# Expert choice: router logits from rows not normed yet, and the first gather issued a stage earlier

## The chip, the cores and the metric

One core of a Trainium2 chip runs the whole program in one launch. The metric is the device time of one execution in microseconds (us). The median of three runs stands for a kernel; one further execution was profiled.

## The reference, cut to what matters

The program is a model of a first block and a second block of two layers. All is float32; there are 1024 tokens of 1024 features. Each layer of the second block ends in this:

```
x   = layer_norm(ALPHA * x + mix, ln_mix_g, ln_mix_b)      # mix = a @ w_o
aff = softmax(x @ w_router, axis=-1)                       # 1024 x 16
gates, idx = top_k(aff.T, 128)                             # 128 tokens for each of 16 experts
out = silu(x[idx] @ w_g) * (x[idx] @ w_u) @ w_down * gates
ffn = zeros.at[idx].add(out)
x   = layer_norm(ALPHA * x + ffn, ln_ffn_g, ln_ffn_b)
```

The last product of the mixing, `a @ w_o`, the first layer norm, the router and the choice of tokens are one stage of the kernel. The experts are the next.

## The kernel before, in words

`layer_tail` runs twice, as `ec0` for the first layer and as `ec1` for the second. It calls `product_and_choose` (names `ec0p`, `ec1p`) and then `choice_phase` (`ec0e`, `ec1e`). Each is a block of its own: every engine has its own list of instructions in a fixed order, engines wait for each other by semaphores, and all engines meet at the end of a block.

**product_and_choose** goes over 8 tiles of 128 tokens. For tile t:

- TensorE makes the product in two halves of 512 columns (`product`, L2840), eight float32 matmuls each, which the trace shows as 16 records. Between them it transposes the previous tile's normed rows `o` (`transposes`, L2849) and, from tile 2 on, turns the affinities of the tile before that (`turn_aff`, L2867). After the second half it makes the previous tile's router logits (`logits`, L2860).
- VectorE adds the residual (`total`, L2963), norms (`normed`, L2969 to L2983), does the softmax (`softmax`, L2988 to L2993) and keeps the turned affinities (`keep_aff`, L2999).
- ScalarE squares and roots (`square_and_root`), does the Exp (`exps`), copies the transposed rows out of PSUM (`keep_x`, L2923), and issues the stores of `o` and of ALPHA times `o` (`store_o`, `store_acc`). It loads the Exp table and the Sqrt table in turn.
- SyncE loads the residual rows, the norm's vectors, the router's weight, and then the first expert's weights.

The choice of the 128 best tokens is made by 16 rounds of MAX8 and MATCH_REPLACE8 on VectorE (`rounds`, L3007 to L3013), once over tokens 0 to 511 (part 0) and once over the rest (part 1). Part 0 runs in the later tiles, part 1 after the last tile, and then the two lists are merged (L3042 to L3047), transposed by TensorE (L2887, L2888) and cast into `idx` (L3050).

In stretches where TensorE would be idle, `stay_awake` (L35) multiplies an identity matrix by itself: 15 times ahead of the last tile's transposes, 22 times near the end of part 1's rounds, and 16 times at the start of `choice_phase`.

**choice_phase** first copies a column of `idx` and gathers 128 rows of x with an indirect DMA issued by GpSimd (`gather`, L3116). TensorE, after its 16 identity matmuls, transposes them (`turn_x`, L3162), VectorE copies all 1024 columns out of PSUM (`keep_x`, L3303), and the loop over experts begins (L3183).

Of the kernel before, what the change touches and what calls it, by code (L numbers as in the profile page):

```python
# [74 lines left out]
class Phase:  # L75
# [27 lines left out]
    def engine(self, eng, name):  # L103
# [12 lines left out]
            lru_lambda_2=16)  # L116
# [2614 lines left out]
class Layers:  # L2731

    def __init__(self, ph, ahead):
# [10 lines left out]
        self.tile_out = ph.sem("tile_out")  # L2744


def layer_tail(nc, outer, name, layers, wo_in, ln_mix, w_router, w_gu, w_dn, x_dram, mid_dram, acc_dram, ln_ffn, out_dram, steps, end):

    with Phase(nc, name, into=outer) as ph:
        gate = ph.sb("gate", [P, E2])  # L2750
        idx = ph.sb("idx", [P, E2], U32)
        weights = Experts(ph, w_gu, w_dn, layers.wd)
        with Phase(nc, f"{name}p") as one:
            product_and_choose(nc, one, layers, layers.aT, layers.ident, wo_in, ln_mix, w_router, x_dram, mid_dram, acc_dram, gate, idx, weights, ln_ffn,
                               steps, end)
        choice_phase(nc, ph, f"{name}e", layers, mid_dram, acc_dram, gate, idx, weights, ln_ffn, out_dram, steps, end)


def product_and_choose(nc, ph, layers, aT, ident, wo_in, ln_mix, w_router, x_dram, mid_dram, acc_dram, gate, idx, weights, ln_ffn, steps, end):
# [7 lines left out]
    junk = ph.sb("junk", [P, D])  # L2767
    warm = ph.sb("warm", [P, NT + 1])
    xT = ph.sb("xT", [P, 2, KD, P])
    small = ph.sb("small", [P, 2, 8])  # L2770
# [16 lines left out]
    def lanes(part, n):  # L2787
# [8 lines left out]
             "a_kept acc_ready tops f_psum cleared near_end").split()  # L2796
    (consts, half_psum, summed, nm_ready, sq_done, ms_ready, root, o_half, x_psum, xT_ready, l_psum, sh_ready, exp_done, aff_ready, a_psum,
     a_kept, acc_ready, tops, f_psum, cleared, near_end) = [ph.sem(n) for n in names]
# [6 lines left out]
    with nc.Block() as block:  # L2805

        @block.sync
        def _(sp):
# [23 lines left out]
        def _(pe):  # L2832

            def product(t, h):
                if t == 0:
                    pe.wait_ge(wo_in[h], 32)
                if t >= 2:
                    pe.wait_ge(summed, 2 * (t - 2) + h + 1)
                for k in range(KD):
                    m = nc.tensor.matmul(po[:, t % 2, halves[h]], aT[:, k, t * P:(t + 1) * P], wo[:, k, halves[h]], start=k == 0, stop=k == KD - 1)  # L2840
                m.then_inc(half_psum, 1)

            def transposes(t):
                for h in range(2):
                    pe.wait_ge(o_half, 2 * t + h + 1)
                    if t:
                        pe.wait_ge(xT_ready, 2 * (t - 1) + h + 1)
                    for k in range(4 * h, 4 * h + 4):
                        m = nc.tensor.transpose(pt[:, k * P:(k + 1) * P], o[:, t % 2, k * P:(k + 1) * P], ident[:, :])  # L2849
                    m.then_inc(x_psum, 1)  # L2850

            def logits(t):
                if t == 0:
                    pe.wait_ge(consts, 48)
                else:
                    pe.wait_ge(exp_done, t)
                for k in range(KD):
                    if k % 4 == 0:
                        pe.wait_ge(xT_ready, 2 * t + k // 4 + 1)
                    m = nc.tensor.matmul(pl[:, 0:E2], xT[:, t % 2, k, :], w[:, k, :], start=k == 0, stop=k == KD - 1)  # L2860
                m.then_inc(l_psum, 1)
# [7 lines left out]
            for t in range(NT):  # L2869
                product(t, 0)  # L2870
                if t >= 2:
# [11 lines left out]
            pe.wait_ge(exp_done, NT)  # L2883
# [7 lines left out]
        @block.gpsimd  # L2891
        def _(pool):
            for part in range(2):
                nc.gpsimd.memset(top[part][:, :], 0.0)
                for j in range(PER):
                    m = nc.gpsimd.memset(state[part][j], 0.0)
                m.then_inc(cleared, 1)

        @block.scalar
        def _(act):  # L2900
# [8 lines left out]
            def exps(t):  # L2909
                u = t % 2  # L2910
                act.wait_ge(sh_ready, t + 1)
                if t >= 2:
                    act.wait_ge(aff_ready, t - 1)
                nc.scalar.activation(ex[:, u, :], pl[:, 0:E2], ACT.Exp, bias=soft[:, u, 0:1], accum_out=soft[:, u, 1:2]).then_inc(exp_done, 1)
                if t < NT - 1:
                    nc.scalar.activation(warm[:, t:t + 1], ident[:, 0:1], ACT.Sqrt)

            def keep_x(t):
                for h in range(2):
                    act.wait_ge(x_psum, 2 * t + h + 1)  # L2920
                    if t >= 2:
                        act.wait_ge(l_psum, t - 1)
                    nc.scalar.copy(xT[:, t % 2, 4 * h:4 * h + 4, :], pt[:, halves[h]].rearrange("p (k t) -> p k t", k=4)).then_inc(xT_ready, 1)  # L2923
# [11 lines left out]
            for t in range(NT):  # L2935
                square_and_root(t)
                if t:
                    exps(t - 1)
                store_o(t)
                if t < NT - 1:  # L2940
                    store_acc(t)
                keep_x(t)
            nc.scalar.activation(warm[:, NT - 1:NT], ident[:, 0:1], ACT.Exp)
            exps(NT - 1)
            store_acc(NT - 1)
# [8 lines left out]
        def _(dve):  # L2954
# [11 lines left out]
            def normed(t):  # L2966
# [3 lines left out]
                dve.wait_ge(nm_ready, t + 1)  # L2970
                if t >= 2:
                    dve.wait_ge(o_out[u], 16 * (t // 2))
                    dve.wait_ge(x_psum, 2 * (t - 1))
                    dve.wait_ge(acc_ready, t - 1)
                if t == 0:
                    dve.wait_ge(consts, 48)
# [5 lines left out]
                for h in range(2):  # L2982
                    nc.vector.scalar_tensor_tensor(o[:, u, halves[h]], o[:, u, halves[h]], small[:, u, 6:7], gb[:, 1, halves[h]], ALU.mult, ALU.add).then_inc(o_half, 1)  # L2983

            def softmax(t):
                u = t % 2
                dve.wait_ge(l_psum, t + 1)
                nc.vector.reduce_max(soft[:, u, 0:1], pl[:, 0:E2], AX_X, negate=True).then_inc(sh_ready, 1)  # L2988
# [4 lines left out]
                nc.vector.tensor_scalar(aff[:, :], ex[:, u, :], soft[:, u, 2:3], None, ALU.mult).then_inc(aff_ready, 1)  # L2993

# [21 lines left out]
            between = {5: (range(0, 0), range(0, 6)), 6: (range(6, 9), range(9, 12)), 7: (range(12, 14), range(14, 16))}  # L3016
            total(0, 0)
            total(0, 1)
            for s in range(1, NT + 1):
                if s > 1:  # L3020
                    total(s - 1, 1)
                normed(s - 1)
                if s >= 2:
                    softmax(s - 2)
                if s in between and between[s][0]:
                    rounds(0, between[s][0])
                if s < NT:
                    total(s, 0)
                if s >= 2:
                    keep_aff(s - 2)  # L3030
                if s in between and between[s][1]:
                    rounds(0, between[s][1])
# [16 lines left out]
            for g in range(NGR):  # L3049
                nc.vector.tensor_copy(idx[32 * g:32 * g + WIDE, 0:E2], pl[0:WIDE, 32 * g:32 * g + E2])  # L3050


def choice_phase(nc, outer, name, layers, x_dram, acc_dram, gate, idx, weights, ln_ffn, out_dram, steps, end):
# [13 lines left out]
    with Phase(nc, name, into=outer) as ph:  # L3067
        wg, wd, wg_in, wd_in = weights.wg, weights.wd, weights.wg_in, weights.wd_in
        ic = [ph.sb(f"ic{v}", [P, 1], U32) for v in range(2)]
        xg = ph.sb("xg", [P, D])  # L3070
# [11 lines left out]
        names = "ic_ready x_in x_psum x_ready g_used half_psum silu hid_ready h_psum hT_a hT_v d_used y_ready sent added".split()  # L3082
        (ic_ready, x_in, x_psum, x_ready, g_used, half_psum, silu, hid_ready, h_psum, hT_a, hT_v, d_used, y_ready, sent,
# [8 lines left out]
        with nc.Block(no_gpsimd_drain=True) as block:  # L3092
# [19 lines left out]
            def _(pool):  # L3112
# [6 lines left out]
                pool.wait_ge(ic_ready, 2)  # L3119
                gather(0)  # L3120
# [34 lines left out]
            def _(pe):  # L3155
# [11 lines left out]
                turn_x()  # L3167
# [53 lines left out]
            def _(act):  # L3221
# [39 lines left out]

                with act.Fori(0, LAST) as e:
# [34 lines left out]
            def _(dve):  # L3297
                V.open(hT_v, x_ready, y_ready)
                V.open(hid_ready, n=2)
                dve.wait_ge(x_psum, 2)  # L3300
# [3 lines left out]

                keep_x()
# [484 lines left out]
def moe_and_transformer_kernel(nc, I, out):  # L3790
# [10 lines left out]
    with ExitStack() as routes:  # L3801
# [23 lines left out]
        with Phase(nc, "layers") as both:  # L3825
            layers = Layers(both, ahead)
# [39 lines left out]
```

## Time and profile before

| | |
|---|---|
| median of 3 runs | 4438.68 us (4438.11 to 4441.31) |
| the profiled execution | 4434.76 us, its span 4433.0 us |
| mean granted TensorE clock | 0.986 |
| busy share of the span | TensorE 96%, its weight loads 50%, VectorE 35%, ScalarE 24%, GpSimd 6% |
| part of the chain that ended last | TensorE 15% of the span, all else near 0% |

Times in the profile count from the start of the span. A busy TensorE is one with matmuls under way; float32 matmuls appear as two records each, and records overlap, so the distance between starts says more than a record's own length.

### The profile page before, as it was taken

What the parts mean: (1) busy time and instruction counts of PE and PEld (TensorE: products, weight loads), DVE (VectorE), ACT (ScalarE), POOL (GpSimd) and SP (SyncE); (2) the same over time, 40 slices, a digit from 0 to 9 for tenths busy, and PEclk for the clock granted to TensorE, in tenths of its full rate; (3) what the DMA queues carried; (4) which work ended last, traced back from release to release, by engine and by line L of the source; (5) the groups of instructions that cost most, each with busy time, mean ns of one, the idle gap of its engine ahead of it and who ended that gap; (6) DMA issues with size and microseconds to landing.
All of it is one profiled execution on the core that took longest, in us unless ns stands there. A gap on an engine that the chain in (4) does not pass through costs nothing. (4 is left out here: it accounts for less than half of the span.)

```text
span 4433.0 us, 62622 instructions
## 1 busy us (share of the span) xinstructions
PE 4248.5 (96%) x23844; PEld 2232.4 (50%) x23845; DVE 1561.6 (35%) x2869; ACT 1083.2 (24%) x1861; POOL 276.7 (6%) x326
## 2 busy tenths in 40 slices
PE   9999999998999999989898899999999997999998
PEld 6555446777445644454554444444444454444443
DVE  4564564443432422233756201010456444011013
ACT  1364223444210011111643000000346331000002
POOL 0000002221000010010000000000000000000000
PEclk9999999999999999999999999999999998999999
DMA  2300155332322699940114688989511144988896
GB/s 87 149 27 31 43 214 131 91 91 64 132 100 84 221 361 360 347 167 19 39 68 185 224 314 314 319 306 318 173 35 34 62 185 175 317 307 321 308 321 244
DMA packets 411747, 807.84 MB, mean 182 GB/s; under 512 B 140944, under 2 KB 276112, under 8 KB 378640
## 3 DMA queue, kind: packets, MB, share of 16 engines
q1 hardware_dynamic: 382496, 704.01, 45.5%
q0 software_dynamic: 16848, 61.35, 4.7%
q10 hardware_dynamic: 12192, 39.46, 2.2%
q8 instruction: 158, 2.59, 0.2%
q14 instruction: 53, 0.43, 0.0%
HBM read 682.77 MB, written 121.63 MB: 181 GB/s over the span
## 5 line engine op out<-in xcount | busy, mean ns | idle before, releaser
L3183 PE MATMUL ec1e_pg<-ec_wg,ec1e_xT 128*128 128x512 f32 x1024 | 443.8, 594 | 2.1 <-DVE ec1e_xT L3303 2.1
L3183 PE MATMUL ec0e_pg<-ec_wg,ec0e_xT 128*128 128x512 f32 x1024 | 442.1, 592 | 2.1 <-DVE ec0e_xT L3303 2.1
L3183 PEld LDWEIGHTS ec1e_pg<-ec_wg,ec1e_xT 128*128 128x128 f32 x1024 | 195.1, 191 | 247.8 <-issue 247.8
L3183 PEld LDWEIGHTS ec0e_pg<-ec_wg,ec0e_xT 128*128 128x128 f32 x1024 | 194.5, 190 | 246.7 <-issue 246.7
L3211 PE MATMUL ec0e_py<-late_wd,ec0e_hidT 128*128 128x512 f32 x512 | 226.2, 594 | 3.4 <-ACT ec0e_hidT L3239 3.4
L3211 PE MATMUL ec1e_py<-late_wd,ec1e_hidT 128*128 128x512 f32 x512 | 226.2, 594 | 3.4 <-ACT ec1e_hidT L3239 3.4
L3539 PE MATMUL lrui_pA<-lrui_xT,lrui_w 128*128 128x512 f32 x512 | 221.3, 592 | 1.4 <-DVE lrui_xT L3692 1.4
L785 PE MATMUL front_pz<-h_h_all,h_w 128*128 128x512 f32 x480 | 209.5, 594 | 3.2 <-PEq L91 3.2
L3234 ACT ACTIVATE ec1e_sg<-ec1e_pg 128x512 f32<-128x512 f32 x32 | 19.1, 597 | 599.0 <-PE ec1e_pg L3183 599.0
L3234 ACT ACTIVATE ec0e_sg<-ec0e_pg 128x512 f32<-128x512 f32 x32 | 19.1, 597 | 598.8 <-PE ec0e_pg L3183 598.8
L3311 DVE TENSOR_TENSOR ec1e_hid<-ec1e_sg,ec1e_pg 128x512 f32<-128x512 f32 x32 | 22.0, 688 | 399.5 <-ACT ec1e_sg L3234 399.5
L3311 DVE TENSOR_TENSOR ec0e_hid<-ec0e_sg,ec0e_pg 128x512 f32<-128x512 f32 x32 | 22.0, 688 | 398.3 <-ACT ec0e_sg L3234 398.3
L3539 PEld LDWEIGHTS lrui_pA<-lrui_xT,lrui_w 128*128 128x128 f32 x512 | 97.2, 190 | 124.2 <-issue 124.2
L1124 POOL TENSOR_TENSOR wkv_a_l<-wkv_a_raw,linear_tab 128x512 f32<-128x512 f32 x80 | 106.4, 1361 | 791.1 <-ACT wkv_a_raw L1143 791.1
L3211 PEld LDWEIGHTS ec0e_py<-late_wd,ec0e_hidT 128*128 128x128 f32 x512 | 94.7, 190 | 113.9 <-issue 113.9
L3211 PEld LDWEIGHTS ec1e_py<-late_wd,ec1e_hidT 128*128 128x128 f32 x512 | 94.7, 190 | 113.9 <-issue 113.9
L785 PEld LDWEIGHTS front_pz<-h_h_all,h_w 128*128 128x128 f32 x480 | 90.5, 190 | 120.2 <-issue 120.2
L534 PE MATMUL mlaa_pS<-mla_kT,mla_qT 96*128 96x512 f32 x256 | 123.8, 606 | 6.5 <-ACT mlaa_probs L598 4.5
L1337 PE MATMUL wkv_bZ<-h_h_all,h_w 128*128 128x512 f32 x240 | 126.6, 612 | 1.5 <-PEq L91 1.5
L3568 PE MATMUL lrui_pB<-late_wd,lrui_gw 128*128 128x512 f32 x256 | 116.4, 613 | 6.5 <-ACT lrui_buf L3608 6.5
L2840 PE MATMUL ec1p_po<-late_wd,layers_aT 128*128 128x512 f32 x256 | 112.7, 594 | 1.7 <-PEq L91 1.7
L2840 PE MATMUL ec0p_po<-late_wd,layers_aT 128*128 128x512 f32 x256 | 112.7, 594 | 1.7 <-PEq L91 1.7
(690 smaller groups left out, 6446.6 us busy)
## 6 DMA issues: line engine op xcount, KB each, us to landing
ec_wg<-in_moe_w_gate_up_dram SPq DMA_DIRECT2D x256, 1024.0 KB, 6.7
late_wd<-in_moe_w_down_dram SPq DMA_DIRECT2D x256, 512.0 KB, 4.5
moe_wb<-in_w_dram SPq DMA_DIRECT2D x32, 1024.0 KB, 12.1
h_h_all<-in_w_dram SPq DMA_DIRECT2D x32, 1024.0 KB, 11.9
yb<-mlaa_zero SPq DMA_DIRECT2D x1, 16384.0 KB, 43.1
moe_w2b<-in_w_dram SPq DMA_DIRECT2D x16, 1024.0 KB, 12.2
mixed_mixT<-in_w_dram SPq DMA_DIRECT2D x16, 1024.0 KB, 12.4
yb<-ahead_rows ACTq DMA_DIRECT2D x32, 512.0 KB, 7.8
```

The source lines that it names most:

```text
L534: m = nc.tensor.matmul(pS[:, u % 2 * 2 + j, :], q_all[:, head, tile * P:(tile + 1) * P], k_all[:, head, j * HALF:(j + 1) * HALF], start=Tr ...
L785: m = nc.tensor.matmul(pz[q % 2][:, half * HALF:(half + 1) * HALF], w[:, q % U, k, :], hT[:, k, half * HALF:(half + 1) * HALF], start=k == ...
L1124: nc.gpsimd.tensor_tensor(grid(a_l[:, n, :]), grid(a_raw[:, :]), mask(n + 1), ALU.mult).then_inc(a_masked, 1)
L1337: m = nc.tensor.matmul(bZ[:, :], gate_w[:, slot, k, :], hT[:, k, halves[g % 2]], start=k == 0, stop=k == KD - 1)
L2840: m = nc.tensor.matmul(po[:, t % 2, halves[h]], aT[:, k, t * P:(t + 1) * P], wo[:, k, halves[h]], start=k == 0, stop=k == KD - 1)
L3183: return nc.tensor.matmul(pg[:, b, :], xT[:, k, :], wg[:, k, b * HALF:(b + 1) * HALF], start=k == 0, stop=k == KD - 1)
L3211: m = nc.tensor.matmul(py[:, b * HALF:(b + 1) * HALF], hidT[:, k, :], wd[:, k, b * HALF:(b + 1) * HALF], start=k == 0, stop=k == KD - 1)
L3234: nc.scalar.activation(sg[:, half * HALF:(half + 1) * HALF], pg[:, half, :], ACT.Silu).then_inc(silu, 1)
L3311: nc.vector.tensor_tensor(hid[:, cols], sg[:, cols], pg[:, 2 + half, :], ALU.mult).then_inc(hid_ready, 1)
L3539: m = nc.tensor.matmul(pA[:, bank, :], w[:, q % W_RING, k, :], xT[:, k, halves[h]], start=k == 0, stop=k == KD - 1)
L3568: m = nc.tensor.matmul(pB[:, at, :], gw[:, u % 2, z, k, c, :], xc[:, u // 2 * 2 + c, halves[h]], start=c == 0, stop=c == 1)
```

## The change

The router is applied to the rows before they are normed. With r the unnormed row, m its mean, s the reciprocal root and g, b the norm's vectors, the logits of the normed row are

logits = s * (r @ (g*W) - m * colsum(g*W)) + colsum(b*W).

- New in the stage: two small loads of g and b by columns (`gb_cols`, from a vector table that grows by 32 columns), two VectorE products for `wz` (`columns`), 8 float32 matmuls with a matrix of ones (`column_sums`) after tile 0's product, their copy (`keep_sums`), and two VectorE operations of 128x16 for each tile in `softmax`.
- `transposes` reads `r` instead of `o` and waits for `summed`. It is cut in halves: half 0 of a tile goes between the quarters of that same tile's second product half, half 1 into the next tile. The product is issued in four pieces. `logits` of a tile goes into the middle of the next tile, and `turn_aff` comes one tile earlier than before.
- After the last product: half of the logits, the second half of the transposes (its copy now by VectorE), the other half of the logits, softmax. The norm's final scaling of the last tile is put around the softmax. The 15 identity matmuls there are gone; the 22 and the 16 stay.
- The rounds of part 0 are spread anew over the tiles 4 to 7.
- The first gather is issued by GpSimd in the product stage, straight from `idx`, after the stores of `o` have landed. This block ends with GpSimd's drain, as before.
- In `choice_phase` the first transposes signal after each half; VectorE copies half 0, ScalarE half 1, and TensorE waits for ScalarE's (`x_late`) ahead of the loop.

```diff
@@ product_and_choose, SyncE
+            for n, name in enumerate(("ln_mix_g_2", "ln_mix_b_2")):
+                at = vec_at(name)[0] + (KD if end else 0)
+                sp.dma_start(gb_cols[:, n, :], layers.vecs[:, at:at + KD]).then_inc(consts, 16)
@@ TensorE
             for t in range(NT):
-                product(t, 0)
-                if t >= 2:
-                    turn_aff(t - 2)
-                if t >= 1:
-                    transposes(t - 1)
-                product(t, 1)
-                if t >= 1:
-                    logits(t - 1)
-            stay_awake(nc, pt[:, 0:P], ident, 15)
-            turn_aff(NT - 2)
-            transposes(NT - 1)
-            logits(NT - 1)
+                product(t, 0, 0)
+                if t:
+                    transposes(t - 1, 1)
+                product(t, 0, 1)
+                if t:
+                    logits(t - 1, 0)
+                    logits(t - 1, 1)
+                product(t, 1, 0)
+                if t:
+                    turn_aff(t - 1)
+                transposes(t, 0)
+                product(t, 1, 1)
+                if t == 0:
+                    column_sums()
+            logits(NT - 1, 0)
+            transposes(NT - 1, 1)
+            logits(NT - 1, 1)
             turn_aff(NT - 1)
@@ GpSimd
+            for u in range(2):
+                pool.wait_ge(o_out[u], 16 * (NT // 2))
+            pool.wait_ge(idx_ready, NGR)
+            pool.indirect_dma_start(first_x[:, :], None, mid_dram, bass.IndirectOffsetOnAxis(ap=idx[:, 0:1], axis=0)).then_inc(first_in, 16)
@@ VectorE
-            between = {5: (range(0, 0), range(0, 6)), 6: (range(6, 9), range(9, 12)), 7: (range(12, 14), range(14, 16))}
...
+            early = {5: range(2, 4), 6: range(8, 10), 7: range(13, 14)}
+            late = {5: range(4, 8), 6: range(10, 13), 7: range(14, 16)}
+            columns()
             total(0, 0)
+            for t in range(1, NT):
+                total(t - 1, 1)
+                normed(t - 1)
+                if t == 1:
+                    keep_sums()
+                if t in early:
+                    rounds(0, early[t])
+                total(t, 0)
+                softmax(t - 1)
+                if t in late:
+                    rounds(0, late[t])
+                keep_aff(t - 1)
+                if t == 4:
+                    rounds(0, range(0, 2))
+            total(NT - 1, 1)
+            minus_mean(NT - 1)
+            last_half()
+            centre(NT - 1)
             softmax(NT - 1)
@@ choice_phase, TensorE
                 pe.wait_ge(x_in, 16)
-                turn_x()
+                for h in range(2):
+                    for k in range(4 * h, 4 * h + 4):
+                        t = nc.tensor.transpose(pt[:, k * P:(k + 1) * P], xg[:, k * P:(k + 1) * P], ident[:, :])
+                    t.then_inc(x_psum if h else x_first, 1)
+                pe.wait_ge(x_late, 1)
```

## Rows read from the trace of the kernel before

**Rows 1.** Windows of stages: us, busy by engine, granted clock, DMA share, GB/s
```profile
2288.80:2416.24 127.44, 127.44 (x414) 65.58 (x415) 62.66 (x150) 44.62 (x74) 3.86 (x10) 1.00 0.47 178
2416.24:2427.68 11.44, 9.08 (x73) 8.28 (x71) 5.64 (x18) 8.34 (x15) 0.00 (x0) 0.88 0.91 314
2427.68:2456.22 28.54, 7.37 (x46) 7.08 (x46) 26.64 (x64) 0.64 (x4) 0.00 (x0) 0.57 0.15 59
2456.22:2466.56 10.34, 6.31 (x41) 6.14 (x41) 1.23 (x1) 1.49 (x2) 2.30 (x4) 0.83 0.18 52
...
3671.38:3682.50 11.12, 8.77 (x73) 7.98 (x71) 5.63 (x17) 8.34 (x15) 0.00 (x0) 0.94 0.84 311
```

**Rows 2.** Timeline of ec0p's tile 7: start, length, what
```profile
2408.39 0.27 PE L2867 MATMUL ec0p_pa<-late_ident,ec0p_aff 128*16 128x128 f32 x1
...
2408.50 1.04 PE L2849 MATMUL ec0p_pt<-late_ident,ec0p_o 128*128 128x128 f32 x8
...
2409.37 7.03 PE L2840 MATMUL ec0p_po<-late_wd,layers_aT 128*128 128x512 f32 x16
```

**Rows 3.** Timeline of ec0p after its last product
```profile
2416.24 1.85 PE L2860 MATMUL ec0p_pl<-ec0p_w,ec0p_xT 128*128 128x16 f32 x16
...
2416.52 0.69 DVE L2963 SCALAR_TENSOR_TENSOR ec0p_r<-ec0p_xt,ec0p_po 128x512 f32<-128x512 f32 x1 [0.64 <-PE ec0p_po L2840]
...
2417.25 0.21 DVE L2969 TENSOR_SCALAR ec0p_small<-ec0p_small 128x1 f32<-128x1 f32 x1
...
2417.50 1.28 DVE L2977 SCALAR_TENSOR_TENSOR ec0p_o<-ec0p_r,ec0p_small,ec0p_gb 128x1024 f32<-128x1024 f32 x1
...
2419.47 1.42 DVE L2983 SCALAR_TENSOR_TENSOR ec0p_o<-ec0p_o,ec0p_small,ec0p_gb 128x512 f32<-128x512 f32 x2
...
2422.01 1.05 PE L2849 MATMUL ec0p_pt<-late_ident,ec0p_o 128*128 128x128 f32 x8
...
2422.79 1.05 ACT L2923 COPY ec0p_xT<-ec0p_pt 128x512 f32<-128x512 f32 x2
...
2423.86 1.28 ACT L2943 ACT_TABLE_LOAD   x1
2425.16 0.20 ACT L2943 ACTIVATE ec0p_warm<-late_ident 128x1 f32<-128x1 f32 x1
...
2425.98 0.28 ACT L2914 ACTIVATE ec0p_ex<-ec0p_pl,ec0p_soft 128x16 f32<-128x16 f32 x1 [0.62 <-DVE ec0p_soft L2988]
...
2426.58 0.23 DVE L2993 TENSOR_SCALAR ec0p_aff<-ec0p_ex,ec0p_soft 128x16 f32<-128x16 f32 x1
```

**Rows 4.** DMA issues of ec1p: KB, us to landing
```profile
ec1p_w<-in_moe_w_router_dram SPq DMA_DIRECT2D x1, 64.0 KB, 7.9
```

**Rows 5.** VectorE groups by line and shape: busy, mean ns
```profile
L2268 DVE COPY ahead_rows<-exp_py 128x512 f32<-128x512 f32 x32 | 22.1, 691 | 39.2 <-PE exp_py L2190 38.7 <-issue 0.3
...
L2517 DVE TENSOR_TENSOR gqap_rr<-gqap_qs,ahead_tab 128x128 f32<-128x128 f32 x32 | 7.2, 287 | 1.2
```

**Rows 6.** Timeline from the cast of idx to the experts, ec0e and ec1e
```profile
2458.18 5.44 PE L35 MATMUL ec0e_pg<-late_ident 128*128 128x128 f32 x32 [2.70 <-PEq L91]
...
3713.39 3.81 PE L35 MATMUL ec1e_pg<-late_ident 128*128 128x128 f32 x32 [2.53 <-PEq L91]
3713.43 1.00 POOL L3116 DMA_INDIRECT ec1e_xg<-x,ec1e_ic  x1 [0.48 <-POOL ec1e_ic L3118]
...
3717.82 1.09 PE L3162 MATMUL ec1e_pt<-late_ident,ec1e_xg 128*128 128x128 f32 x8 [0.61 <-DMA ec1e_xg<-x,ec1e_ic]
3718.95 1.23 DVE L3303 COPY ec1e_xT<-ec1e_pt 128x1024 f32<-128x1024 f32 x1 [7.34 <-PE ec1e_pt L3162]
...
3720.96 1.85 PE L3183 MATMUL ec1e_pg<-ec_wg,ec1e_xT 128*128 128x512 f32 x3 [2.05 <-DVE ec1e_xT L3303]
```

**Rows 7.** Timeline of an earlier stage that ends with a gather in flight
```profile
1511.39 0.94 POOL L1817 DMA_INDIRECT moe_xg<-h,moe_idx  x1 [0.30 <-issue]
...
1513.15 2.92 PE L35 MATMUL exp_pg<-h_ident 128*128 128x128 f32 x24 [1.17 <-PEq L1784]
```

More of the change, by code:

```diff
@@ L2731, with __init__ @@
 class Layers:
-    def __init__(self, ph, ahead):
+    def __init__(self, ph, ahead, vecs):
         self.ident, self.wd = ahead.ident, ahead.wq
@@ L2751, in layer_tail @@
         idx = ph.sb("idx", [P, E2], U32)
+        xg = ph.sb("xg", [P, D])
+        x_in = ph.sem("x_in")
         weights = Experts(ph, w_gu, w_dn, layers.wd)
@@ L2754, in layer_tail, with product_and_choose @@
             product_and_choose(nc, one, layers, layers.aT, layers.ident, wo_in, ln_mix, w_router, x_dram, mid_dram, acc_dram, gate, idx, weights, ln_ffn,
-                               steps, end)
-        choice_phase(nc, ph, f"{name}e", layers, mid_dram, acc_dram, gate, idx, weights, ln_ffn, out_dram, steps, end)
-def product_and_choose(nc, ph, layers, aT, ident, wo_in, ln_mix, w_router, x_dram, mid_dram, acc_dram, gate, idx, weights, ln_ffn, steps, end):
+                               steps, end, xg, x_in)
+        choice_phase(nc, ph, f"{name}e", layers, mid_dram, acc_dram, gate, idx, weights, ln_ffn, out_dram, steps, end, xg, x_in)
+def product_and_choose(nc, ph, layers, aT, ident, wo_in, ln_mix, w_router, x_dram, mid_dram, acc_dram, gate, idx, weights, ln_ffn, steps, end, first_x,
+                       first_in):
     wo = weights.wd
@@ L2766, in product_and_choose @@
     o = ph.sb("o", [P, 2, D])
-    junk = ph.sb("junk", [P, D])
+    junk = first_x
     warm = ph.sb("warm", [P, NT + 1])
     xT = ph.sb("xT", [P, 2, KD, P])
+    ones = ph.sb("ones", [P, P])
+    gb_cols = ph.sb("gb_cols", [P, 2, KD])
+    wz = ph.sb("wz", [P, KD, 2, E2])
+    col_sums = ph.sb("col_sums", [P, 2, E2])
+    z = ph.sb("z", [P, 2, E2])
     small = ph.sb("small", [P, 2, 8])
@@ L2832, in _ @@
         def _(pe):
-            def product(t, h):
-                if t == 0:
-                    pe.wait_ge(wo_in[h], 32)
-                if t >= 2:
-                    pe.wait_ge(summed, 2 * (t - 2) + h + 1)
-                for k in range(KD):
[L2840 to L2861, printed above, removed]
+            def product(t, h, part):
+                if part == 0:
+                    if t == 0:
+                        pe.wait_ge(wo_in[h], 32)
+                    if t >= 2:
+                        pe.wait_ge(summed, 2 * (t - 2) + h + 1)
+                for k in range(4 * part, 4 * part + 4):
+                    m = nc.tensor.matmul(po[:, t % 2, halves[h]], aT[:, k, t * P:(t + 1) * P], wo[:, k, halves[h]], start=k == 0, stop=k == KD - 1)
+                if part:
+                    m.then_inc(half_psum, 1)
@@ new lines, in column_sums, with transposes @@
+            def column_sums():
+                pe.wait_ge(ones_set, 1)
+                pe.wait_ge(wz_ready, 1)
+                for k in range(KD):
+                    m = nc.tensor.matmul(pa[:, 0:2 * E2], ones[:, :], wz[:, k, :, :].rearrange("p n e -> p (n e)"), start=k == 0, stop=k == KD - 1)
+                m.then_inc(sums_psum, 1)
+            def transposes(t, h):
+                pe.wait_ge(summed, 2 * t + h + 1)
+                if t:
+                    pe.wait_ge(xT_ready, 2 * (t - 1) + h + 1)
+                for k in range(4 * h, 4 * h + 4):
+                    m = nc.tensor.transpose(pt[:, k * P:(k + 1) * P], r[:, t % 2, k * P:(k + 1) * P], ident[:, :])
+                m.then_inc(x_psum, 1)
@@ L2863, in turn_aff, with logits @@
+            def logits(t, h):
+                if t and h == 0:
+                    pe.wait_ge(sh_ready, t)
+                pe.wait_ge(xT_ready, 2 * t + h + 1)
+                for k in range(4 * h, 4 * h + 4):
+                    m = nc.tensor.matmul(pl[:, 0:E2], xT[:, t % 2, k, :], wz[:, k, 0, :], start=k == 0, stop=k == KD - 1)
+                if h:
+                    m.then_inc(l_psum, 1)
             def turn_aff(t):
@@ L2892, in _ @@
         def _(pool):
+            nc.gpsimd.memset(ones[:, :], 1.0).then_inc(ones_set, 1)
             for part in range(2):
@@ L2913, in exps, with keep_x @@
                     act.wait_ge(aff_ready, t - 1)
-                nc.scalar.activation(ex[:, u, :], pl[:, 0:E2], ACT.Exp, bias=soft[:, u, 0:1], accum_out=soft[:, u, 1:2]).then_inc(exp_done, 1)
+                nc.scalar.activation(ex[:, u, :], z[:, u, :], ACT.Exp, bias=soft[:, u, 0:1], accum_out=soft[:, u, 1:2]).then_inc(exp_done, 1)
                 if t < NT - 1:
                     nc.scalar.activation(warm[:, t:t + 1], ident[:, 0:1], ACT.Sqrt)
[L2918 to L2923, printed above, removed]
+            def keep_x(t, h):
+                act.wait_ge(x_psum, 2 * t + h + 1)
+                if t >= 2 and h == 0:
+                    act.wait_ge(l_psum, t - 1)
+                nc.scalar.copy(xT[:, t % 2, 4 * h:4 * h + 4, :], pt[:, halves[h]].rearrange("p (k t) -> p k t", k=4)).then_inc(xT_ready, 1)
             def store_o(t):
@@ L2934, in _ @@
             nc.scalar.activation(warm[:, NT:NT + 1], ident[:, 0:1], ACT.Sqrt)
[L2935 to L2942, printed above, removed]
+            keep_x(0, 0)
+            for t in range(1, NT):
+                square_and_root(t - 1)
+                keep_x(t - 1, 1)
+                store_o(t - 1)
+                store_acc(t - 1)
+                exps(t - 1)
+                keep_x(t, 0)
+            square_and_root(NT - 1)
             nc.scalar.activation(warm[:, NT - 1:NT], ident[:, 0:1], ACT.Exp)
             exps(NT - 1)
+            store_o(NT - 1)
             store_acc(NT - 1)
@@ L2981, in normed, with scale, last_half @@
                 V.link(nc.vector.reciprocal(small[:, u, 6:7], small[:, u, 5:6]))
-                for h in range(2):
-                    nc.vector.scalar_tensor_tensor(o[:, u, halves[h]], o[:, u, halves[h]], small[:, u, 6:7], gb[:, 1, halves[h]], ALU.mult, ALU.add).then_inc(o_half, 1)
+            def scale(t, h):
+                u = t % 2
+                nc.vector.scalar_tensor_tensor(o[:, u, halves[h]], o[:, u, halves[h]], small[:, u, 6:7], gb[:, 1, halves[h]], ALU.mult, ALU.add).then_inc(o_half, 1)
+            def normed(t):
+                minus_mean(t)
+                centre(t)
+                scale(t, 0)
+                scale(t, 1)
+            def last_half():
+                dve.wait_ge(x_psum, 2 * NT)
+                nc.vector.tensor_copy(xT[:, (NT - 1) % 2, 4:KD, :], pt[:, halves[1]].rearrange("p (k t) -> p k t", k=4)).then_inc(xT_ready, 1)
             def softmax(t):
@@ L2987, in softmax @@
                 dve.wait_ge(l_psum, t + 1)
-                nc.vector.reduce_max(soft[:, u, 0:1], pl[:, 0:E2], AX_X, negate=True).then_inc(sh_ready, 1)
+                V.link(nc.vector.scalar_tensor_tensor(z[:, u, :], col_sums[:, 0, :], small[:, u, 2:3], pl[:, 0:E2], ALU.mult, ALU.add))
+                V.link(nc.vector.scalar_tensor_tensor(z[:, u, :], z[:, u, :], small[:, u, 6:7], col_sums[:, 1, :], ALU.mult, ALU.add))
+                nc.vector.reduce_max(soft[:, u, 0:1], z[:, u, :], AX_X, negate=True).then_inc(sh_ready, 1)
+                if t == NT - 1:
+                    scale(t, 0)
                 dve.wait_ge(exp_done, t + 1)
@@ L3014, in rounds, with columns, keep_sums @@
                                                        state[part][j][at, :], -1.0))
-            between = {5: (range(0, 0), range(0, 6)), 6: (range(6, 9), range(9, 12)), 7: (range(12, 14), range(14, 16))}
-            total(0, 0)
[L3018 to L3032, printed above, removed]
+            def columns():
+                dve.wait_ge(consts, 80)
+                for n in range(2):
+                    c = nc.vector.tensor_tensor(wz[:, :, n, :], w[:, :, :], gb_cols[:, n, :].unsqueeze(2).to_broadcast([P, KD, E2]), ALU.mult)
+                c.then_inc(wz_ready, 1)
+            def keep_sums():
+                dve.wait_ge(sums_psum, 1)
+                V.link(nc.vector.tensor_copy(col_sums[:, :, :], pa[:, 0:2 * E2].rearrange("p (n e) -> p n e", n=2)))
+            early = {5: range(2, 4), 6: range(8, 10), 7: range(13, 14)}
+            late = {5: range(4, 8), 6: range(10, 13), 7: range(14, 16)}
+            columns()
+            total(0, 0)
+            for t in range(1, NT):
+                total(t - 1, 1)
[15 more added lines that the diff above has]
+            centre(NT - 1)
             softmax(NT - 1)
@@ L3049, in _, with choice_phase @@
             for g in range(NGR):
-                nc.vector.tensor_copy(idx[32 * g:32 * g + WIDE, 0:E2], pl[0:WIDE, 32 * g:32 * g + E2])
-def choice_phase(nc, outer, name, layers, x_dram, acc_dram, gate, idx, weights, ln_ffn, out_dram, steps, end):
+                nc.vector.tensor_copy(idx[32 * g:32 * g + WIDE, 0:E2], pl[0:WIDE, 32 * g:32 * g + E2]).then_inc(idx_ready, 1)
+def choice_phase(nc, outer, name, layers, x_dram, acc_dram, gate, idx, weights, ln_ffn, out_dram, steps, end, xg, x_in):
     LAST, R, FIRST, MIDDLE = E2 - 1, NT + 1, 4, 5
@@ L3166, in _ @@
                 pe.wait_ge(x_in, 16)
-                turn_x()
+                for h in range(2):
+                    for k in range(4 * h, 4 * h + 4):
+                        t = nc.tensor.transpose(pt[:, k * P:(k + 1) * P], xg[:, k * P:(k + 1) * P], ident[:, :])
+                    t.then_inc(x_psum if h else x_first, 1)
+                pe.wait_ge(x_late, 1)
                 def one_expert(e, more):
@@ L3260, in roots @@
                     nc.scalar.activation(small[:, t, 4:5], small[:, t, 3:4], ACT.Sqrt).then_inc(root, 1)
+                act.wait_ge(x_psum, 2)
+                nc.scalar.copy(xT[:, 4:KD, :], pt[:, HALF:D].rearrange("p (k t) -> p k t", k=4)).then_inc(x_late, 1)
                 with act.Fori(0, LAST) as e:
@@ L3825, in moe_and_transformer_kernel @@
         with Phase(nc, "layers") as both:
-            layers = Layers(both, ahead)
+            layers = Layers(both, ahead, I["vecs"])
             gqa_phase(nc, layers, ahead, I["attn_w_qkv_2"], I["attn_sink_2"], I["gqa_masks"], (slots, weights, x1, yb, x2), I["attn_w_o_2"],
```

32 lines of the change are left out of this document (16 added, 16 removed).

## The prediction

> **What bounds the kernel now.** I read the page first: TensorE is busy 96% of the span and the chain that ended last runs through it, so time is saved or lost where TensorE gains work, waits, or stands idle. Then I cut the stages that the change touches into windows [rows 1], layer ec0 in full. The reader is to see four stretches. The product stage, 127.44 us, is TensorE without a gap at full clock, with VectorE busy for half of it. The tail, 11.44 us, goes from the last product's end (I call it E, 2416.24) to the first round of part 1. The rounds, 28.54 us, have VectorE busy 26.64 us, and TensorE at half clock (0.57 on the mean). The boundary, 10.34 us, goes from `idx` cast to the first expert matmul. In the first stretch a removed TensorE instruction is a gain and an added one a loss; in the other three only the chain of dependences counts. The second layer's tail is 11.12 us. A timeline of each stretch gives the parts.
>
> A check of the first stretch: 16 product records take 6.87 us (2409.37 to 2416.24), so eight tiles are 16 x 6.87 = 109.9 us. A turned affinity costs 0.11 us (2408.39 to 2408.50) and a tile's eight transposes 0.87 us (to 2409.37) [rows 2]. A tile's logits, 16 records in 1.85 us, overlap by some 0.15 with what follows: 1.7 us [rows 3]. With 7 transposed tiles, 6 logits and 6 turns the stage should be 109.9 + 6.1 + 10.2 + 0.7 = 126.9, and 127.44 is left: about 0.02 us for each of some 27 changes from one kind of matmul to another. The model holds, so I use it for the new stage.
>
> **Product stage, for each layer.** It is TensorE's own sum that counts.
> - The logits of tile 6 stood behind E before; now those of tiles 0 to 6 all stand ahead of it: +1.7 us. This is a move, and the tail must pay it back.
> - Column sums, 8 float32 matmuls of 128x32 with full weight loads: the nearest row is a tile's logits (128x16, also 16 records): +1.7 us. It could be 1.7 to 2.1 for the double width.
> - Half a tile more of transposes, +0.44, and one more turn, +0.11.
> - Some 18 more changes of kind: +0.4 us at 0.02 each; 0 to 1.
> - A new wait at the start. `columns` stands ahead of `total(0,0)` on VectorE and waits for five loads. The router's weight, issued at 3545.7 in ec1, takes 7.9 us [rows 4] and lands at 3553.6; the two column loads are queued behind it and small, so some 0.5 us later, 3554.1. Two products of 128x128 at 0.287 us [rows 5] and a total of 0.73 (2416.52 to 2417.25) [rows 3] end at 3555.5. TensorE wants half 0 of tile 0's transposes after three quarters of its first product, 10.3 us after 3543.9, at 3554.2. It waits 1.3 us. How fast the small loads land behind the large ones is the unknown; between nothing and 2.5 us I take 0.9 for either layer. Behind the waiting transposes stands all of TensorE's list, so the wait counts in full.
>
> Sum: +5.3 us (bounds +3.9 to +7.9). Nothing else should make TensorE wait. In the new order VectorE has 16.5 us for a tile and needs in tile 5, its fullest, two totals (1.5), the norm (3.6), the softmax with its two new operations (some 1.8 with waits), the copy (0.3) and six rounds of about 1.5: 16.2 us, with waits about 17.4. The lateness, 0.9 us, is less than the 3.4 us that a quarter of the product gives ahead of the transposes that need `total(5,1)`. ScalarE has slack: 44.62 us busy of 127.
>
> **Tail, for each layer**, from E. Before, `total` ends and the mean's sum starts at E + 1.01. Now TensorE begins the last four transposes there, E + 1.05. From a start of transposes to the copy of the first four is 0.78 us (2422.01 to 2422.79): VectorE copies at E + 1.83. The copy is 0.69 [rows 5], to E + 2.52. The centring follows; from its start to that of the scaling, with root and reciprocal in between, is 1.97 us (2417.50 to 2419.47), so E + 4.5. The last half of the logits is long there. Three small operations of about 0.2 us end at E + 5.2. But ScalarE can load the Exp table only after the root, which is some 0.2 us ahead of that, at about E + 4.3: 1.28 for the load and 0.20 for the warming one put Exp at E + 5.8, and this is what sets it. From Exp to the affinities is 0.60 us (2425.98 to 2426.58): E + 6.4. Before, 1.10 us passed from there to the first round; now half the scaling, 0.75 (half of the pair of 1.42, and its overlap), stands in between, under which the turn is hidden: 1.5 us. First round at E + 7.95 [rows 3]. Against 11.44 and 11.12, mean 11.3 [rows 1], this gives back 3.3 us (2.3 to 4). The 15 identity matmuls that go were off this chain: TensorE waits for affinities behind them.
>
> ScalarE's table load is where the Trainium skill speaks against the change. The trace has 1.28 us for the load and the next activation 0.02 us behind it (2423.86, 2425.16) [rows 3]. The page "ScalarE: Activation LUTs", section "What ACT_TABLE_LOAD costs", gives a further 1.38 us of drain for every switch of set. By it Exp would come at E + 7.2, and the sum at the end would be 2.8 us higher. The trace does not show such a drain around these loads, so I go by the trace.
>
> **Rounds**: the same 16 rounds, merge and casts, the same 22 identity matmuls; 0.
>
> **Boundary, for each layer.** Before, TensorE starts its 16 identity matmuls 1.96 us after `idx` (2458.18 against 2456.22) [rows 1, 6]. They last 5.44 us at a clock that is low for part of it, and in ec1 3.81 us. The gather, issued at 3713.43, lets the transposes start at 3717.82, 4.4 us later, and ec1's waited 0.6 us for it. So the early gather can win 0.6 us in one layer and nothing in the other, where the identity matmuls end last. Against that, GpSimd now spends 1.0 us on the issue before all engines meet. An earlier stage ended so: its last gather was issued from 1511.39 to 1512.33, and TensorE's next matmul came at 1513.15 [rows 7]. By that TensorE starts 0.1 + 1.0 + 0.8 = 1.9 us after `idx`, as before; with the full 1.96 after the issue, 1.1 us later. I take +0.5, less 0.3 for the gather in ec1: +0.2 (bounds -0.6 to +1.1). The split copy: before, 3.14 us from the transposes' start to the first expert matmul (3717.82 to 3720.96), of which 0.8 passes after the copy's end. Now ScalarE's half ends some 1.8 us after the start, and the loop is entered behind the wait instead of under it: 0.8 to 1.3 more. Gain 0.3 (0 to 0.6).
>
> **Sum**: +5.3 - 3.3 + 0 + 0.2 - 0.3 = +1.9 us a layer, +3.8 for two, which I round to +4. The profiled execution was 4434.76 us (its span 4433.0 and 1.8 around it); 3.9 us under the median. 4438.7 + 4 = 4442.7, say 4443. Less than 0.2%, 8.9 us, is about what a measurement of this kernel can't tell from no change. The rest of the program is untouched but for a vector table 32 columns wider.
>
> **The rivals.**
> - *The drain waits for the rows (slower; the other side of my forecast).* This block ends with GpSimd's drain; the stage of [rows 7] has none. If it holds GpSimd till the gather lands, all engines meet 4.4 us after the issue instead of 1.0: TensorE's identity matmuls start 3.4 us later still. 4443 + 6.8 = 4450. From about 2.5 us of drain it decides. Nothing in the trace shows it for or against, as no such block had a gather in flight. 13 in 100.
> - *VectorE gets late (slower).* If the new order makes TensorE wait 0.5 us in each of seven tiles, the layers pay 7 us: 4450. For it: TensorE now waits for the total of the same tile, with one quarter between. Against it: the slack of 3.4 us worked out above. 7 in 100.
> - *The tail pays more, and the clock helps (faster).* If wait and changes of kind cost nothing (-1.3 a layer), the tail ends at E + 7.3 (-0.7), and the identity matmuls of both boundaries run at full clock (1.6 us in ec0), the total is about 1.6 us under before: 4437. To be faster by 0.2% it needs 4.5 us a layer under before, which only a longer part of the rounds moved into the product stage would give, and they are not moved. 5 in 100 for faster by 0.2%.
> - *Neither the early gather nor the split does anything*, because the identity matmuls end last and the loop's entry takes what the copy gave: +0.6 a layer, 4444. This lies within the forecast.
>
> **Numbers.** The likeliest case, with its rival of no effect, holds 75 in 100, from 4434 to 4448. Both slower rivals and an unnamed rest of slower ones make 20, faster ones 5. The range 4434 to 4452 leaves out the far ends of both. Faster by over 0.2%: 0.05; within: 0.75; slower: 0.20.
>
> **What would show it.** The product stage from first matmul to E should be 132 to 133.5 us, with a gap ahead of the first transposes of 0.5 to 1.5; E to the first MAX8 of part 1 about 8 us, with Exp right behind a table load and its warming; the rounds 28 to 29 us; `idx` to the first expert matmul 9.2 to 10.6. I would be wrong if TensorE shows gaps inside tiles 1 to 7, if GpSimd's issue is followed by more than 2 us without an engine starting, or if the stage of products grows by under 3 us.

## The result, and the profile after

The changed kernel takes 4449.27 us (median of 11 runs, 4444.2 to 4455.73) against 4438.68 before: a ratio of 1.0023, 95% interval 1.0015 to 1.0031. It is slower by 0.23%; the interval lies wholly above 1, so the loss is beyond the noise, although the forecast took anything under 0.2% for about no change. The forecast was 4443 and the range 4434 to 4452.

The windows of the same stretches in the changed kernel, ec0 first, then ec1 (us, busy by engine, granted clock, DMA share, GB/s):

```profile
2294.91:2426.49 131.58, 131.58 (x451) 69.35 (x452) 68.03 (x171) 49.81 (x80) 4.01 (x11) 1.00 0.45 173
2426.49:2433.89 7.40, 3.06 (x22) 2.34 (x20) 5.84 (x17) 3.26 (x8) 0.00 (x0) 0.88 0.84 317
2433.89:2462.88 28.99, 7.78 (x46) 7.54 (x46) 26.64 (x64) 1.66 (x5) 0.00 (x0) 0.56 0.28 101
2462.88:2477.87 14.99, 6.09 (x41) 5.91 (x41) 0.69 (x2) 1.59 (x2) 2.18 (x4) 0.77 0.12 36
3554.66:3686.25 131.59, 131.58 (x451) 69.28 (x452) 68.04 (x171) 49.83 (x80) 4.03 (x11) 1.00 0.45 169
3686.25:3693.66 7.41, 3.11 (x22) 2.34 (x20) 5.83 (x16) 3.22 (x7) 0.00 (x0) 0.86 0.81 302
3693.66:3722.55 28.89, 7.63 (x46) 7.40 (x46) 26.65 (x65) 1.70 (x5) 0.00 (x0) 0.56 0.29 105
3722.55:3737.34 14.79, 6.17 (x40) 5.99 (x41) 0.70 (x2) 1.63 (x2) 2.24 (x4) 0.77 0.13 37
```

Against [rows 1], ec0: the product stage is 4.1 us longer, the tail 4.0 shorter, the rounds 0.45 longer, the boundary 4.65 longer, together +5.2. For ec1 the other windows of before are these:

```profile
3543.93:3671.38 127.45, 127.45 (x415) 65.58 (x416) 62.67 (x150) 44.61 (x74) 3.87 (x10) 1.00 0.46 174
3682.50:3711.61 29.11, 7.94 (x46) 7.70 (x46) 26.65 (x64) 0.65 (x4) 0.00 (x0) 0.56 0.15 62
3711.61:3720.96 9.35, 4.90 (x40) 4.53 (x41) 1.23 (x1) 1.49 (x2) 2.33 (x4) 1.00 0.19 56
```

There the differences are +4.1, -3.7, -0.2 and +5.4, together +5.6. Both layers give 10.8 us, and the medians differ by 10.6. The profiled executions differ by 15.0 (4449.74 against 4434.76), 6.1 of which has passed before ec0 starts (2294.9 against 2288.8). This is not the change: over the profiles of this study ec0 starts between 2288.0 and 2297.8, and both ends belong to variants of the kernel before. So the four windows decide and not the whole span.

The boundary in ec0, from the changed kernel's timeline; "PEq" and "POOLq" are the engines' own queues:

```profile
2462.13 0.75 DVE L3112 CAST ec_idx<-ec0p_pl 32x16 uint32<-32x16 f32 x4 [0.86 <-PE ec0p_pa L2911]
2463.69 0.97 POOL L2925 DMA_INDIRECT ec_xg<-x,ec_idx  x1 [164.77 <-DVE ec_idx L3112]
2469.42 0.19 POOL L3179 COPY ec0e_ic<-ec_idx 128x1 uint32<-128x1 uint32 x1 [4.77 <-POOLq L91]
...
2470.14 5.21 PE L35 MATMUL ec0e_pg<-late_ident 128*128 128x128 f32 x32 [8.04 <-PEq L91]
2475.18 1.04 PE L3228 MATMUL ec0e_pt<-late_ident,ec_xg 128*128 128x128 f32 x8
...
2477.87 2.38 PE L3246 MATMUL ec0e_pg<-ec_wg,ec0e_xT 128*128 128x512 f32 x5 [1.65 <-issue]
```

GpSimd is done with the issue at 2464.66 and does nothing for 4.8 us. The gather lands 4.3 us after its issue, at 2468.0, and GpSimd's next instruction comes 1.4 us behind that. TensorE starts its identity matmuls 7.3 us after `idx`, where it was 2.0 [rows 1, 6]. The rows have been there for two microseconds by then, and still the 5.2 us of identity matmuls stand ahead of them.

### The profile page after: what moved, and what is told of

It is laid out like the page before. It is cut to its first block and busy times, and to the rows that moved or that the text cites. A ratio compares the mean times of both kernels' runs of the same rounds, so it can differ in the third digit from the quotient of the medians.

```text
span 4447.7 us, 62592 instructions
## 1 busy us (share of the span) xinstructions
PE 4251.1 (96%) x23816; PEld 2233.7 (50%) x23817; DVE 1571.6 (35%) x2909; ACT 1085.8 (24%) x1861; POOL 276.9 (6%) x328
```

## The experiments

In the table, "layers" is the sum, over both layers, of the time from the first product matmul to the first expert matmul, and the middle columns are ec0's windows. These times come from one profiled execution each. Each ratio is to the kernel before on the same chip; its medians there were 4438.68 for the changed kernel, 4438.91 for e1 to e4, 4436.29 for e5 to e8 and 4437.76 for e9.

| run | median us | ratio, 95% interval | product | tail | rounds | boundary | layers |
|---|---|---|---|---|---|---|---|
| before | 4438.68 | | 127.4 | 11.4 | 28.5 | 10.3 | 354.8 |
| changed | 4449.27 | 1.0023 [1.0015, 1.0031] | 131.6 | 7.4 | 29.0 | 15.0 | 365.6 |
| e1_no_drain | 4443.02 | 1.0007 [0.9999, 1.0016] | 131.6 | 7.4 | 29.0 | 11.2 | 358.3 |
| e2_before_no_drain | 4439.24 | 1.0004 [0.9995, 1.0013] | 127.4 | 11.1 | 29.0 | 10.6 | 355.4 |
| e3_gather_back | 4437.70 | 0.9997 [0.9988, 1.0005] | 131.6 | 7.4 | 28.9 | 10.1 | 355.0 |
| e4_gather_only | 4446.18 | 1.0013 [1.0004, 1.0021] | 127.4 | 11.1 | 29.2 | 15.5 | 366.8 |
| e5_five_awake | 4435.62 | 0.9995 [0.9986, 1.0005] | 131.6 | 7.4 | 29.0 | 8.8 | 353.4 |
| e6_small_copy | 4439.77 (1 run) | | 127.4 | 11.0 | 28.6 | 13.7 | 362.4 |
| e7_large_copy | 4453.11 (1 run) | | 127.4 | 11.1 | 29.2 | 18.8 | 372.4 |
| e8_before_tuned | 4432.17 | 0.9987 [0.9977, 0.9996] | 127.4 | 11.1 | 29.2 | 8.7 | 353.0 |
| e9_fewer_awake | 4439.98 | 1.0005 [0.9996, 1.0014] | 127.4 | 11.1 | 28.6 | 8.8 | 351.9 |

**e1_no_drain**, the changed kernel:

```diff
-    with nc.Block() as block:
+    with nc.Block(no_gpsimd_drain=True) as block:
```

> The changed kernel with one edit: the product stage's block ends without GpSimd's drain, as the choice stage's block does. Theory A (the drain holds all engines until the first gather has landed): GpSimd's next copy comes about 1.4 us after the end of the gather's issue and not 4.8 us, TensorE's identity matmuls start about 2 us after the issue and not 5.5, so each layer gets back 3 to 4 us and the kernel lands 6 to 8 us under the changed one, near 4442. Rival B (all engines are late because the gather is issued late, 0.8 us after idx, and its issue takes 1 us, whatever the drain): no change, 4449.

Its timeline at ec0's boundary:

```profile
2457.51 0.75 DVE L3112 CAST ec_idx<-ec0p_pl 32x16 uint32<-32x16 f32 x4 [0.87 <-PE ec0p_pa L2911]
2459.07 0.97 POOL L2925 DMA_INDIRECT ec_xg<-x,ec_idx  x1 [164.78 <-POOLq L2814]
2460.89 0.19 POOL L3179 COPY ec0e_ic<-ec_idx 128x1 uint32<-128x1 uint32 x1 [0.85 <-POOLq L91]
...
2461.51 5.44 PE L35 MATMUL ec0e_pg<-late_ident 128*128 128x128 f32 x32 [4.04 <-PEq L91]
```

GpSimd goes on 0.85 us after the issue instead of 4.77. The layers take 7.4 us less, and the median is 6.3 under the changed one's. Theory A stands, rival B falls. What is left: TensorE starts 3.2 us after `idx` and not 2.0. The issue (0.8 us after `idx`, 1.0 long) now lies ahead of the meeting of all engines, which would account for it.

**e2_before_no_drain**, the same edit on the kernel before.

> The kernel before with the same edit, no drain at the end of the product stage's block; no gather is in flight there. Theory A: the drain costs nothing when GpSimd has no transfer under way, so within 1 us of the kernel before, 4438. Rival: the drain has a price of its own at every block end, then 0.5 to 3 us faster.

The layers take 355.4 against 354.8 and the median is within the interval: a drain without a transfer under way costs nothing that can be seen.

**e3_gather_back**, the changed kernel with the gather in the choice stage again (the diff is cut):

```diff
@@ product stage, GpSimd
-            for u in range(2):
-                pool.wait_ge(o_out[u], 16 * (NT // 2))
-            pool.wait_ge(idx_ready, NGR)
-            pool.indirect_dma_start(first_x[:, :], None, mid_dram, ...)
@@ choice stage, GpSimd
                 nc.gpsimd.tensor_copy(ic[0][:, :], idx[:, 0:1]).then_inc(ic_ready, 1)
+                pool.wait_ge(ic_ready, 2)
+                gather(0)
```

> The changed kernel with the first gather put back into the choice stage; the new logits, the new order and the split copy stay. Theory A: the rewritten product stage costs 4.1 us a layer, the shorter tail gives 4.0 back, the split copy 0.4, so this is equal to the kernel before within 2 us, 4438, and 9 to 11 us under the changed one. Rival (the new logits and the order of the product stage carry the loss): 4446 or more.

It is the kernel before again in time: layers 355.0 against 354.8, median 1.2 us under it and within the interval. The new logits, the rebuilt order and the split copy cancel out.

**e4_gather_only**, the kernel before with the early gather alone, from `idx`, the drain kept.

> The kernel before with the early gather alone, issued in the product stage from idx, the block's drain kept. Theory A: the boundary from idx to the first expert matmul grows by some 4.5 us in each layer, so 8 to 10 us slower than before, near 4448. Rival (the early gather is harmless and the loss lies in the logits): 4437 to 4439.

Ec0's timeline:

```profile
2460.35 0.97 POOL L2904 DMA_INDIRECT ec_xg<-x,ec_idx  x1 [164.74 <-DVE ec_idx L3057]
2466.10 0.19 POOL L3124 COPY ec0e_ic<-ec_idx 128x1 uint32<-128x1 uint32 x1 [4.78 <-POOLq L91]
```

Layers +12 us, boundary 15.5 in ec0 and 16.5 in ec1, and GpSimd is silent for 4.78 us as in the changed kernel. The median is 7.3 above the before of its chip, a little under what was expected, with an interval of 1.8 to 9.3 us. The +12 of the one profiled execution lies outside that interval, and why is open. The changed kernel loses 10.8 us in the layers; here as much is lost without any of the new logits.

**e6_small_copy and e7_large_copy**: does the drain wait for landing, or does any transfer make it long? The kernel before, and GpSimd issues one more copy, HBM to HBM, once `idx` is cast; 128 KB in the one (16 rows), 2 MB in the other (256 rows):

```diff
+            pool.wait_ge(idx_ready, NGR)
+            pool.dma_start(layers.extra[int(end), 0:16, :], weights.w_gu[E2 - 1, 0:16, :]).then_inc(layers.extra_in, 16)
```

> The kernel before with one more transfer issued by GpSimd once idx is cast, in the product stage: 128 KB copied from one place of HBM to another, which nobody needs before the end of the choice stage; the drain at the block's end kept. Theory A (the drain waits until the transfers of GpSimd's queue have landed): the choice stage starts after that landing, 2 to 4 us later than before. Rival C (having issued any transfer makes the drain take a fixed time of about 4 us): the same start as in the next run.

> The same with 2 MB instead of 128 KB. Theory A: the choice stage starts only when the 2 MB have landed, 6 to 12 us after their issue, so 4 us or more later than with 128 KB. Rival C (fixed time) or rival D (the drain waits for the issue alone): the same start as with 128 KB.

The small copy lands 2.2 us after its issue in ec0, the large one 8.0. Ec0's timeline with the small copy:

```profile
2455.39 0.55 POOL L2900 DMA_DIRECT2D extra<-in_moe_w_gate_up_dram  x1 [163.49 <-DVE ec_idx L3053]
2459.18 0.19 POOL L3121 COPY ec0e_ic<-ec_idx 128x1 uint32<-128x1 uint32 x1 [3.24 <-POOLq L91]
```

and with the large one:

```profile
2462.76 0.55 POOL L2900 DMA_DIRECT2D extra<-in_moe_w_gate_up_dram  x1 [164.24 <-DVE ec_idx L3053]
2472.31 0.19 POOL L3121 COPY ec0e_ic<-ec_idx 128x1 uint32<-128x1 uint32 x1 [8.99 <-POOLq L91]
```

The landing comes 5.8 us later and GpSimd's next instruction 5.8 us later (9.55 against 3.79 us after the issue). In ec1 it is the same: landings after 2.3 and 8.1 us, next instruction 3.4 and 9.2 us after the issue. The drain waits for the landing; rivals C and D fall.

**e5_five_awake**, e1 with fewer identity matmuls at the start of the choice stage:

```diff
-                stay_awake(nc, pg[:, 0, 0:P], ident, 16)
+                stay_awake(nc, pg[:, 0, 0:P], ident, 5)
```

> The changed kernel without GpSimd's drain at the end of the product stage, and with 5 identity matmuls at the start of the choice stage instead of 16. In the run without the drain the identity matmuls started 3.2 us after idx and ended last; the gather lands about 5.1 us after idx. Theory A (the identity matmuls now hide the early gather's gain): the first expert matmul comes 8 to 8.5 us after idx, against 11.1, so 2.5 to 3 us a layer are gained and the kernel lands 5 us under that run and 1 to 3 us under the kernel before. Rival (fewer identity matmuls leave TensorE at half clock into the first expert): the records of the first expert start 0.85 us apart instead of 0.43 for some microseconds, and 1.5 us or more of each layer's gain is lost again.

Boundary 8.8 and 8.7 us against 11.2: the gain is there, 2.4 us a layer, a little under the 2.5 to 3 expected. The median is 0.7 us under the kernel before, which is not told from no change. The transposes are made partly at half clock, the experts start at full clock; the windows of transposes and first expert:

```profile
2467.80:2470.80 3.00, 1.99 (x11) 1.75 (x10) 0.69 (x1) 0.96 (x2) 0.20 (x1) 0.73 0.00 0
2470.80:2473.80 3.00, 2.39 (x6) 1.23 (x7) 0.00 (x0) 1.11 (x2) 0.75 (x1) 1.00 0.45 124
```

**e8_before_tuned**, the kernel before with the early gather, no drain, the split copy and 5 identity matmuls, and its own logits and order.

> The kernel before, its logits and order kept, with the early gather, no drain, the split copy of the first rows and 5 identity matmuls at the start of the choice stage. Theory A (the new logits are worth nothing on balance, the boundary is what can be won): equal to the run with five identity matmuls within 2 us, 1 to 3 us under the kernel before. Rival (the new logits help once the boundary is mended): 2 us or more above that run.

It is the only run clearly under the kernel before: 4432.17, ratio 0.9987 [0.9977, 0.9996]. Its layers take 353.0 us, those of e5 353.4. The new logits have shown no gain: the rival, which wanted this run 2 us or more above e5, falls. The median is 3.5 us under e5's, more than the 2 us that theory A allowed, while the layers differ by only 0.4; the two ratios' intervals overlap, so whether the new logits cost something outside the layers is open.

**e9_fewer_awake**, e8 with 18 identity matmuls instead of 22 near the end of the rounds, and 3 instead of 5.

> The run of the tuned kernel before, with 18 identity matmuls near the end of the rounds instead of 22 and 3 at the start of the choice stage instead of 5. In that run the 22 ended some 0.5 us after the merge that they should wait for, and 5 ended about when the gather had landed. Theory A: the stretch of rounds gets 0.4 us shorter, the boundary 0 to 0.4, so 0 to 1.6 us in all, about 4431 where the tuned one had 4432. Rival: with fewer of them TensorE is still at half clock when the experts start, so the boundary stays 8.7 us or the first expert's records start 0.85 us apart, and nothing is gained or up to 3 us lost.

The stretch of rounds is 0.6 us shorter in both layers, as meant. But these are the windows of ec0's transposes and of the first expert's start:

```profile
2465.40:2468.40 3.00, 1.86 (x8) 1.46 (x8) 0.69 (x1) 1.09 (x2) 0.33 (x1) 0.50 0.00 0
2468.40:2474.40 6.00, 5.43 (x7) 2.37 (x8) 0.00 (x0) 0.98 (x2) 0.62 (x1) 0.50 0.31 87
```

and two of the expert's weight loads:

```profile
2469.95 0.34 PEld L3191 LDWEIGHTS ec0e_pg<-ec_wg,ec0e_xT 128*128 128x128 f32 x1 [0.52 <-issue]
2470.81 0.34 PEld L3191 LDWEIGHTS ec0e_pg<-ec_wg,ec0e_xT 128*128 128x128 f32 x1 [0.52 <-issue]
```

The granted clock is 0.50, the 1.2 GHz level, up to 2474.4, and the weight loads start 0.85 us apart instead of 0.43. Of the 5.4 us after its first matmul (2468.97) half is lost, 2.7 us a layer, outside the "layers" column. The rival stands in the trace. The median is 2.2 us above the kernel before, within the interval, where e8 was 4.1 under the one of its own chip. Two numbers were changed at once, so this run does not say which of them lost the clock.

## Why the prediction came out as it did

The time lies in the range, but by a mechanism that the forecast gave 13 in 100. Its own sum was +4 us and +10.6 was measured, above the 4448 at which its likeliest case ended. The step that failed is the boundary: the early gather was put at +0.2 us a layer, on the ground that all engines would meet right after its issue, and they met only after its landing.

That the rival's 4450 comes within 1 us is in part luck. With it the forecast had +2.0 us for product stage and tail together and +3.3 for the boundary; measured were +0.1 and +0.4, and +4.65 and +5.4. Errors of about 1.7 us a layer cancel. Step by step, per layer:

- **Product stage**, forecast +5.3, measured +4.1. The terms for moved logits, column sums (from 2309.15 to 2310.86, 1.7 us), half transposes and turns held. The wait at the start, put at 0.9, was nothing: tile 0's total ended as TensorE came to need it. The columns were there 9.05 us after the first product matmul, where the forecast had 10.2. This and 0.2 for the changes of kind instead of 0.4 is the difference, and it puts the stage just under the 132 to 133.5 us that the forecast named as its sign. The timeline of the changed kernel's first tile:

```profile
2294.91 10.54 PE L2853 MATMUL ec0p_po<-late_wd,layers_aT 128*128 128x512 f32 x24 [1.69 <-PEq L91]
...
2303.96 0.49 DVE L3066 TENSOR_TENSOR ec0p_wz<-ec0p_w,ec0p_gb_cols 128x128 f32<-128x128 f32 x2 [9.88 <-DMA ec0p_gb_cols<-in_vecs_dram]
2304.37 0.68 DVE L2992 SCALAR_TENSOR_TENSOR ec0p_r<-ec0p_xt,ec0p_po 128x512 f32<-128x512 f32 x1
...
2305.28 0.60 PE L2869 MATMUL ec0p_pt<-late_ident,ec0p_r 128*128 128x128 f32 x4
```

  VectorE waits 9.88 us for the columns, and is done at 2305.06; TensorE goes from product to transposes at 2305.28 without a gap. It is that close: 0.22 us lie between, and in ec1 0.07 (3564.98 to 3565.05), so by these figures a load 0.3 us later would have stopped TensorE.
- **VectorE late in the tiles** (rival, 7 in 100): no gap of TensorE in any tile; the rival fell.
- **Tail**, forecast -3.3, measured -4.0 and -3.7. The chain was the forecast's, ScalarE's Exp behind the table load included:

```profile
2430.31 0.20 ACT L2935 ACTIVATE ec0p_small<-ec0p_small 128x1 f32<-128x1 f32 x1 [1.40 <-DVE ec0p_small L3008]
2430.53 1.28 ACT L2971 ACT_TABLE_LOAD   x1
...
2431.83 0.20 ACT L2971 ACTIVATE ec0p_warm<-late_ident 128x1 f32<-128x1 f32 x1
2431.93 0.29 ACT L2942 ACTIVATE ec0p_ex<-ec0p_z,ec0p_soft 128x16 f32<-128x16 f32 x1
...
2433.89 0.69 DVE L3054 MAX8 ec0p_top<-layers_rows 16x8 f32<-16x512 f32 x1
```

  Root to Exp is 1.62 us, the load with its warming. Exp came 5.4 us after the last product and not 5.8, and the first round 1.96 us behind it and not 2.15. Of the further 1.38 us of drain that the Trainium skill gives for each switch of set ("ScalarE: Activation LUTs", "What ACT_TABLE_LOAD costs") this trace has nothing: the next activation starts 0.02 us behind the load.
- **Rounds**, forecast 0, measured +0.45 and -0.2, by how long the 22 identity matmuls last (7.6 us against 7.1 in ec0, 7.4 against 7.7 in ec1) and hold up the two transposes behind them.
- **Boundary**, the step that failed. The forecast put the early gather at +0.2, taking the end of an earlier stage [rows 7] as its model. But that stage's block has no drain. With the drain, all engines wait until the gather has landed: +4.65 and +5.4 with the split copy's gain already in. The forecast's own sign of being wrong, more than 2 us behind GpSimd's issue without an engine starting, is there with 4.8. Shown by e1 (the drain taken away gives 3.7 us a layer), e4 (the gather alone costs 6 us a layer) and by the two copies (the wait follows the landing time). The rival "the drain waits for the rows" had this mechanism, and its price of 3.4 us for it is near e1's 3.7. A second, smaller miss is left when the drain is gone: e1's boundary is 0.8 us (ec0) and 1.8 us (ec1) longer than before, where the forecast, split copy included, had -0.1. There TensorE starts 3.2 us after `idx` and not 2.0 and 1.8, and ec1's 16 identity matmuls last 5.4 us where they lasted 3.8.
- **The split copy**, forecast -0.3: from the transposes' start to the first expert matmul 2.69 us in ec0 (2475.18 to 2477.87) and 2.73 in ec1, against 3.10 and 3.14 [rows 6] before, so -0.4.
- **The issue after `idx`**: the forecast took 0.1 us, the record starts 0.8 us after the cast's end. A plain copy issued by GpSimd at the same place (e6) started 0.3 us after it.

That the change doesn't pay even without the drain (e1: +3.5 us on the layers) has one more reason, which the forecast's rival "neither does anything" named: identity matmuls placed for the old landing time end last, so the earlier rows are not used. With 5 of them, e5, the layers take 1.4 us less than before.

## What to carry to other kernels

In this kernel a transfer that GpSimd issued early won nothing where the block that starts it ends with GpSimd's drain: all engines then wait for its landing. Look, at every place where work is moved across a stage's end, at what that end waits for, and look in the trace for the issuing engine's silence between its issue and its next instruction. Work that fills an idle stretch (here identity matmuls for the clock) is sized for that stretch, and has to be sized again when what it waits for comes earlier: 16 were too many, 5 served, and 3, together with 4 fewer ahead of them, were too few. And a computation taken off a short serial tail may cost as much on the engine that bounds the long stage: here 4.1 us against 4.0 in one layer and 3.7 in the other.

## What the runs showed that I had not expected

- GpSimd's drain at a block's end waits for the landing of transfers that GpSimd has issued. Its next instruction came 1.4 to 1.6 us behind the landing in ec0 in three cases, with landings 2.2, 4.3 and 8.0 us after the issue, and 1.1 us behind it in ec1 in the same three. Without a transfer under way the drain had no price that could be seen (e2).
- TensorE after about 4 us of idleness and 5 identity matmuls had full clock when the experts started, and after 3 of them, with 1.0 us more idleness for the rows (and 4 fewer identity matmuls a few microseconds earlier), was at the 1.2 GHz level for the first 5.4 us of the expert.
